# Moving the two halves of x by 64 bytes in SBUF, in a one-core transformer kernel

## The chip, the core and the metric

One NeuronCore of a Trainium2 chip runs the whole program in one launch. The metric is device microseconds from start to end of the program, the median of several executions. Before the change it is 1319.07 us (three executions, 1317.32 to 1320.37).

## What is computed

The input is 256 tokens of 1024 features in float32. Eight layers follow one another: two hybrid blocks ("b1": four mixers beside each other), and then twice a feed-forward layer ("f1"), a second kind of mixer block ("mix") and another feed-forward layer ("f2"). Each reads the normalised x, multiplies it by a large weight matrix, does its own work on the result, multiplies that by a second matrix and adds it to x. Cut to what matters:

```
for l in range(2):
    x = x + mixers(rmsnorm(x) @ w_in[l]) @ w_out[l]          # "b1", w_in 1024 x 3584, w_out 1024 x 1024
x = rmsnorm(x)
for l in range(2):
    h = rmsnorm(x);  x = x + (silu(h @ wg) * (h @ wu)) @ wd   # "f1", wg, wu 1024 x 2816, wd 2816 x 1024
    x = x + mixers2(rmsnorm(x) @ w_in_2[l]) @ w_out_2[l]      # "mix"
    h = rmsnorm(x);  x = x + (silu(h @ wg) * (h @ wu)) @ wd   # "f2"
```

## The kernel before

x stays in SBUF with features on the partitions: `x[P, 8, 256]`, where block k holds features 128k to 128k+127 of all 256 tokens. For the products, float32 values are split into two float32r halves, a high and a low one: x into `xh` and `xl`, the weights into `wh` and `wl`, the hidden layer of a feed-forward layer into `hh` and `hl`, the mixers' outputs into `y1`, `y2` and `y2r` (two tiles each). Every product is then three matmuls: high by high, and high by low both ways.

The weights come in 409 units of 128 x 1024 values, in the order of their use, through `wraw` (5 buffers). ScalarE writes `wh` of a unit (line 882), VectorE `wl` (line 1261); there are 6 buffers of each. TensorE then uses the unit's two tiles of 128 x 512 in one of three forms:

- **Token form** (`project_tokens`, lines 457 to 459), the first product of "b1" and "mix": a 128 x 128 block of `xh` or `xl` is stationary and 512 columns of `wh` or `wl` move. 56 tiles a phase, four phases.
- **Feature form** (`project_features`, lines 473 to 475), the first product of a feed-forward layer: 128 x 128 of `wh` or `wl` is stationary and the 256 columns of `xh` or `xl` move. 88 tiles a phase, four phases.
- **Out form** (`project_out`, lines 488 to 490), the second product everywhere: 128 x 128 of `wh` or `wl` is stationary and 256 columns of `hh` or `hl` (44 tiles a phase), or of the mixers' `y` tiles (16 tiles a phase), move.

Feature form and out form issue the same three matmuls in the same order (high by high, then low moving, then `wl` stationary); 12 of them to a tile. A stationary operand that a matmul needs is loaded by a separate weight load (PEld in the profile), which runs while the matmul before it streams. Each engine's program is one fixed list; semaphores alone tie them together. Between the tiles TensorE also does the mixers' small matmuls and transposes (line 531), the sums of squares for the norms (line 544) and, in "mix", eight pairs of matmuls with the forget gate's weights (lines 733 and 734: `xh` and `xl` move, a slice of `ffw` is stationary that begins 32 bytes further on for each pair).

The tiles lie in SBUF one after the other in the order of the `sb(...)` calls, each start rounded up to 32 bytes. In bytes from the start of a partition, taken from the built programs:

```
tile            before   mod 128  mod 256    after    mod 128  mod 256
wraw             16512       0      128      16512        0      128
wh               36992       0      128      36992        0      128
wl               61568       0      128      61568        0      128
x                86144       0      128      86144        0      128
xh               94336       0      128      94400       64      192
xl              102528       0      128     102592       64      192
cst             110720       0      128     110848        0        0
ffw             123552      32      160     123680       32       32
hh, y1, y2      133184      64       64     133312       64      192
y2r             149568      64       64     149696       64      192
hl              155712      64       64     155840       64      192
```

Within a tile, the slices of the big products begin at multiples of 512 bytes, so that a tile's remainder is that of every operand taken from it.

Of the kernel before, what the change touches and what calls it, by code (L numbers as in the profile page):

```python
# [13 lines left out]
P = 128  # L14
# [175 lines left out]
def program(nc, x_in, w_in, par_in, cst_in, lev_in, msk_in, pos_in, rpb_in, lng_in, lnb_in, out):  # L190
    ctx = ExitStack()

    def sb(name, shape, dt=F32, where=None):
        return (where or ctx).enter_context(nc.sbuf_tensor("s_" + name, shape, dt))
# [5 lines left out]
    wh = sb("wh", [P, NS, UNIT], F32R)  # L200
    wl = sb("wl", [P, NS, UNIT], F32R)
    x = sb("x", [P, 8, TOKENS])
    xh = sb("xh", [P, 8, TOKENS], F32R)
    xl = sb("xl", [P, 8, TOKENS], F32R)
    cst = sb("cst", [P, NCST])
    par = sb("par", [P, NPAR])
    mlev = sb("mlev", [P, NLEV], F32R)
# [2034 lines left out]
```

How the kernel before makes its waits and increments, by code:

```python
        def claim(n, name):  # L440
            b, before = plan[n, name]
            if before:
                pe.wait_ge(emptied[b], before)
            return pb[b]
# [1 line left out]
        def project_tokens(n, tile, c, k):  # L446
            u, j = divmod(tile, TPU)
            s = u % NS
            hi, lo = (w[:, s, NCOL * j:NCOL * (j + 1)] for w in (wh, wl))
            if j == 0 or u < SPLIT_UNITS:
                pe.wait_ge(low_done, piece_of(tile))
            if c == 0:
                pe.wait_ge(xl_done, x_parts(n) + k + 1)
            for t in range(2):
                ts = slice(P * t, P * (t + 1))
                o = (claim(n, ("in", c, t)) if k == 0 else psum(n, ("in", c, t)))[:, :]
                pe.matmul(o, xh[:, k, ts], hi, start=k == 0, stop=False)
                pe.matmul(o, xh[:, k, ts], lo, start=False, stop=False)
                pe.matmul(o, xl[:, k, ts], hi, start=False, stop=k == 7).then_inc(main_done, 1)
# [1 line left out]
        def project_features(n, tile, c, k):  # L461
            u, j = divmod(tile, TPU)
            s = u % NS
            if j == 0 or u < SPLIT_UNITS:
                pe.wait_ge(low_done, piece_of(tile))
            if c == 0:
                pe.wait_ge(xl_done, x_parts(n) + k + 1)
            for i in range(2):
# [9 lines left out]
        def project_out(n, tile, q, pair, first, last):  # L478
# [1 line left out]
            s = u % NS  # L480
            if j == 0:
                pe.wait_ge(low_done, piece_of(tile))
            o2 = claim(n, ("out", q)) if first else psum(n, ("out", q))
```

## Time and profile before

| | |
|---|---|
| median of three executions | 1319.07 us |
| the profiled execution's own time | 1318.59 us |
| its span, first to last instruction | 1316.8 us |
| TensorE busy | 1295.8 us, 98% of the span |
| TensorE's weight loads busy | 1219.4 us, 93% |
| VectorE busy | 900.4 us, 68% |
| ScalarE busy | 709.4 us, 54% |
| mean granted TensorE clock | 0.995 of full |

The profiled execution is 0.48 us under the median, and 1.8 us of its time lie outside the span. A matmul's row gives a modelled length (0.28 us for 256 columns) that overlaps the next matmul's, so TensorE's pace is not read from lengths but from how far apart the starts lie, or from how many matmuls fall in a stretch of known length.

### The profile page before, as it was taken

What the parts mean: (1) busy time and instruction counts of PE and PEld (TensorE: products, weight loads), DVE (VectorE), ACT (ScalarE), POOL (GpSimd) and SP (SyncE); (2) the same over time, 40 slices, a digit from 0 to 9 for tenths busy, and PEclk for the clock granted to TensorE, in tenths of its full rate; (3) what the DMA queues carried; (4) which work ended last, traced back from release to release, by engine and by line L of the source; (5) the groups of instructions that cost most, each with busy time, mean ns of one, the idle gap of its engine ahead of it and who ended that gap; (6) DMA issues with size and microseconds to landing.
All of it is one profiled execution on the core that took longest, in us unless ns stands there. A gap on an engine that the chain in (4) does not pass through costs nothing.

```text
span 1316.8 us, 23603 instructions
## 1 busy us (share of the span) xinstructions
PE 1295.8 (98%) x9662; PEld 1219.4 (93%) x9662; DVE 900.4 (68%) x1588; ACT 709.4 (54%) x1149; POOL 157.6 (12%) x207
## 2 busy tenths in 40 slices
PE   9999999999999999999999999999999999999997
PEld 7788878999999988899999999999998889999997
DVE  6988798867665577767666566666547876766652
ACT  7664665645454485556444544444458546544441
POOL 3201500382001100012000020000110001200000
PEclk9999999999999999999999999999999999999999
DMA  8635644555556552335555555555645133655560
GB/s 313 202 103 177 215 144 129 176 186 175 182 178 195 175 176 79 122 120 193 179 191 192 177 192 184 186 192 181 200 148 185 59 133 126 197 176 183 188 195 34
DMA packets 61499, 221.77 MB, mean 168 GB/s; under 512 B 7120, under 2 KB 7376, under 8 KB 61136
## 3 DMA queue, kind: packets, MB, share of 16 engines
q1 hardware_dynamic: 60768, 219.00, 50.3%
q8 instruction: 76, 1.25, 0.4%
q0 software_dynamic: 336, 1.11, 0.3%
q14 instruction: 31, 0.25, 0.1%
q10 hardware_dynamic: 288, 0.16, 0.1%
HBM read 219.20 MB, written 1.05 MB: 167 GB/s over the span
## 4 chain that ended last, share of the span: by engine, by line
PE 81%; DVE 10%; issue 3%; POOL 3%; ACT 1%; DMA 1%; SPq 0%; DVEq 0%; ACTq 0%; POOLq 0%
PE pb L473 13%; PE pb L475 13%; PE pb L474 13%; PE pb L488 7%; PE pb L490 7%; PE pb L489 7%; PE pb L457 5%; PE pb L459 5%; PE pb L458 5%; DVE s_wl L1261 3%; DVE s_acc L1394 2%; PE pb L531 2%; PE pb L581 2%; PE pb L704 1%; PE pb L560 1%
## 5 line engine op out<-in xcount | busy, mean ns | idle before, releaser
L1261 DVE TENSOR_TENSOR s_wl<-s_wraw,s_wh 128x1024 fp32r<-128x1024 f32 (+1 forms) x411 | 503.5, 1245 | 115.1 <-ACT s_wh L882 114.8
L882 ACT ACTIVATE s_wh<-s_wraw 128x1024 fp32r<-128x1024 f32 (+1 forms) x411 | 420.9, 1048 | 201.6 <-PE pb L475 113.2
L473 PE MATMUL pb<-s_xh,s_wh 128*128 128x256 f32 x1408 | 399.8, 284 | 0.0
L475 PE MATMUL pb<-s_xh,s_wl 128*128 128x256 f32 x1408 | 399.1, 283 | 0.0
L474 PE MATMUL pb<-s_xl,s_wh 128*128 128x256 f32 x1408 | 399.0, 283 | 0.0
L473 PEld LDWEIGHTS pb<-s_xh,s_wh 128*128 128x128 f32 x1408 | 271.0, 192 | 0.0
L474 PEld LDWEIGHTS pb<-s_xl,s_wh 128*128 128x128 f32 x1408 | 271.0, 192 | 0.0
L475 PEld LDWEIGHTS pb<-s_xh,s_wl 128*128 128x128 f32 x1408 | 270.9, 192 | 0.0
L488 PE MATMUL pb<-s_hh,s_wh 128*128 128x256 f32 x704 | 194.6, 276 | 0.0
L489 PE MATMUL pb<-s_hl,s_wh 128*128 128x256 f32 x704 | 194.5, 276 | 0.0
L490 PE MATMUL pb<-s_hh,s_wl 128*128 128x256 f32 x704 | 194.5, 276 | 0.0
L457 PE MATMUL pb<-s_wh,s_xh 128*128 128x512 f32 x448 | 183.0, 409 | 1.9 <-DVE s_wl L1261 1.9
L459 PE MATMUL pb<-s_wh,s_xl 128*128 128x512 f32 x448 | 175.9, 393 | 0.0
L458 PE MATMUL pb<-s_wl,s_xh 128*128 128x512 f32 x448 | 175.6, 392 | 0.0
L1598 DVE TENSOR_TENSOR s_gu<-pb,s_rbc 128x512 f32<-128x512 f32 x88 | 60.8, 691 | 116.9 <-PE pb L475 112.4
L489 PEld LDWEIGHTS pb<-s_hl,s_wh 128*128 128x128 f32 x704 | 132.3, 188 | 0.0
L488 PEld LDWEIGHTS pb<-s_hh,s_wh 128*128 128x128 f32 x704 | 132.2, 188 | 0.0
L490 PEld LDWEIGHTS pb<-s_hh,s_wl 128*128 128x128 f32 x704 | 132.2, 188 | 0.0
L457 PEld LDWEIGHTS pb<-s_wh,s_xh 128*128 128x128 f32 x448 | 84.7, 189 | 20.7 <-DVE s_wl L1261 3.1
L459 PEld LDWEIGHTS pb<-s_wh,s_xl 128*128 128x128 f32 x448 | 84.4, 188 | 18.4
L458 PEld LDWEIGHTS pb<-s_wl,s_xh 128*128 128x128 f32 x448 | 84.8, 189 | 14.9
L1070 ACT ACTIVATE s_sg<-s_gu 128x256 f32<-128x256 f32 x88 | 36.7, 420 | 86.2 <-DVE s_gu L1598 86.0
(302 smaller groups left out, 1515.6 us busy)
## 6 DMA issues: line engine op xcount, KB each, us to landing
s_wraw<-in_w SPq DMA_DIRECT2D x407, 512.0 KB, 4.0
s_nab<-in_rpb SPq DMA_DIRECT2D x2, 1024.0 KB, 8.0
s_x<-in_x SPq DMA_DIRECT2D x4, 256.0 KB, 5.9
out_dram<-s_at_s SPq DMA_DIRECT2D x4, 256.0 KB, 2.3
s_cst<-in_cst SPq DMA_DIRECT2D x1, 684.0 KB, 10.3
s_mlev<-in_lev POOLq DMA_DIRECT2D x1, 576.0 KB, 5.3
s_wraw<-in_w SPq DMA_DIRECT2D x2, 256.0 KB, 4.6
s_ln<-in_lng POOLq DMA_DIRECT2D x2, 128.0 KB, 6.3
```

What stands on the lines that cost most here:

```text
L457: pe.matmul(o, xh[:, k, ts], hi, start=k == 0, stop=False)
L458: pe.matmul(o, xh[:, k, ts], lo, start=False, stop=False)
L459: pe.matmul(o, xl[:, k, ts], hi, start=False, stop=k == 7).then_inc(main_done, 1)
L473: pe.matmul(o, wh[:, s, w], xh[:, k, :], start=k == v == 0, stop=False, skip_group_check=True)
L474: pe.matmul(o, wh[:, s, w], xl[:, k, :], start=False, stop=False, skip_group_check=True)
L475: r = pe.matmul(o, wl[:, s, w], xh[:, k, :], start=False, stop=k == 7, skip_group_check=True)
L488: pe.matmul(o, wh[:, s, w], ah, start=first and m == v == 0, stop=False, skip_group_check=True)
L489: pe.matmul(o, wh[:, s, w], al, start=False, stop=False, skip_group_check=True)
L490: r = pe.matmul(o, wl[:, s, w], ah, start=False, stop=last and m == 1, skip_group_check=True)
L882: return act.activation(o, src, ACT.Copy, scale=scale)
L1261: dve.tensor_tensor(wl[:, s, part], wraw[:, r, part], wh[:, s, part].bitcast(F32), ALU.subtract).then_inc(low_done, 1)
L1598: dve.tensor_tensor(gu[:, j, :, :], psum(n, ("in", c, j))[:, :].rearrange("p (a b) -> p a b", a=2), rbc[:, RBC_SLOT[n], :].unsqueeze(1).to ...
```

## The change

Two unused tiles of 64 bytes a partition are put in, one ahead of `xh`, one behind `xl`.

```diff
     x = sb("x", [P, 8, TOKENS])
+    sb("gap0", [P, 16])
     xh = sb("xh", [P, 8, TOKENS], F32R)
     xl = sb("xl", [P, 8, TOKENS], F32R)
+    sb("gap1", [P, 16])
     cst = sb("cst", [P, NCST])
```

`xh` and `xl` then begin 64 bytes further on, everything behind them 128 bytes further on; the table above has both. No instruction, semaphore or DMA is added, removed or moved: on each of the five engines the two built programs list the same instructions in the same order, with the same shapes.

## Rows read from the trace of the kernel before

**Rows 1.** The page's head and its part 1, busy time of each engine

```profile
span 1316.8 us, 23603 instructions
PE 1295.8 (98%) x9662; PEld 1219.4 (93%) x9662; DVE 900.4 (68%) x1588; ACT 709.4 (54%) x1149; POOL 157.6 (12%) x207
```

**Rows 2.** The page's part 5: one group of each form

```profile
L473 PE MATMUL pb<-s_xh,s_wh 128*128 128x256 f32 x1408 | 399.8, 284 | 0.0
L488 PE MATMUL pb<-s_hh,s_wh 128*128 128x256 f32 x704 | 194.6, 276 | 0.0
L457 PE MATMUL pb<-s_wh,s_xh 128*128 128x512 f32 x448 | 183.0, 409 | 1.9 <-DVE s_wl L1261 1.9
```

**Rows 3.** Windows, TensorE alone: length, busy (matmuls touching it), clock, DMA, GB/s

```profile
280.00:388.00 108.00, 108.00 (x903) 1.00 0.55 182
610.00:723.00 113.00, 113.00 (x944) 1.00 0.56 185
389.00:448.00 59.00, 59.00 (x523) 1.00 0.60 192
725.00:783.00 58.00, 58.00 (x514) 1.00 0.62 194
```

**Rows 4.** Timeline of TensorE where a feature stretch ends: start, length, instruction

```profile
388.35 0.28 PE L474 MATMUL pb<-s_xl,s_wh 128*128 128x256 f32 x1
388.47 0.28 PE L475 MATMUL pb<-s_xh,s_wl 128*128 128x256 f32 x1
388.59 0.29 PE L488 MATMUL pb<-s_hh,s_wh 128*128 128x256 f32 x1
...
389.07 0.28 PE L489 MATMUL pb<-s_hl,s_wh 128*128 128x256 f32 x1
389.18 0.28 PE L490 MATMUL pb<-s_hh,s_wl 128*128 128x256 f32 x1
```

**Rows 5.** Windows, TensorE alone, in out form: three mixer stretches, the last feed-forward

```profile
239.00:251.00 12.00, 12.00 (x108) 1.00 0.82 254
122.00:134.00 12.00, 12.00 (x104) 1.00 0.64 216
1109.00:1118.00 9.00, 9.00 (x79) 1.00 0.52 168
1297.30:1305.80 8.50, 8.50 (x75) 1.00 0.00 0
```

**Rows 6.** Windows of all engines: busy of PE, PEld, DVE, ACT, POOL

```profile
8.00:109.00 101.00, 97.51 (x500) 80.24 (x499) 86.36 (x186) 65.14 (x118) 17.32 (x22) 0.99 0.59 201
449.00:568.00 119.00, 118.81 (x668) 98.80 (x667) 86.35 (x255) 74.61 (x132) 7.40 (x10) 1.00 0.37 122
610.00:723.00 113.00, 113.00 (x944) 113.00 (x943) 73.55 (x98) 56.09 (x81) 0.00 (x0) 1.00 0.56 185
```

**Rows 7.** Timeline of TensorE in token form, in the first "mix"

```profile
481.95 0.39 PE L458 MATMUL pb<-s_wl,s_xh 128*128 128x512 f32 x1
482.17 0.39 PE L459 MATMUL pb<-s_wh,s_xl 128*128 128x512 f32 x1
482.40 0.39 PE L457 MATMUL pb<-s_wh,s_xh 128*128 128x512 f32 x1
```

**Rows 8.** Timeline of TensorE in the forget gate's matmuls, about the fourth and eighth pair

```profile
452.68 0.28 PE L734 MATMUL pb<-s_xl,s_ffw 128*128 128x256 f32 x1
452.79 0.28 PE L733 MATMUL pb<-s_xh,s_ffw 128*128 128x256 f32 x1
452.91 0.28 PE L734 MATMUL pb<-s_xl,s_ffw 128*128 128x256 f32 x1
...
453.62 0.29 PE L734 MATMUL pb<-s_xl,s_ffw 128*128 128x256 f32 x1
453.75 0.28 PE L733 MATMUL pb<-s_xh,s_ffw 128*128 128x256 f32 x1
453.87 0.28 PE L734 MATMUL pb<-s_xl,s_ffw 128*128 128x256 f32 x1
```

## The prediction

> **What bounds the kernel now.** I read the page's busy times first: TensorE is busy for 1295.8 of 1316.8 us [rows 1], so the end is set by TensorE's pace and little else. A change that moves no instruction can then act in one way only, by the distance between successive matmul starts. Those distances come from windows: length of a stretch that holds nothing but one form, over the matmuls in it. A window counts all matmuls that touch it, and since a modelled length of 0.28 us spans more than two distances, some 2.5 too many.
>
> Feature form (`xh`, `xl` move, weights stationary): 108.00 us over 903 - 2.5, and 113.00 over 944 - 2.5, give 119.9 and 120.0 ns [rows 3]. Out form of the feed-forward layers (`hh`, `hl` move, weights stationary): 59.00 over 523 - 2.5, and 58.00 over 514 - 2.5, give 113.4 ns for both [rows 3]. Both stream 256 columns against the same weight tiles, in the same order, with the same number of loads. The timeline at the end of a feature stretch shows the switch in place: 0.12 us between starts while `xl` and `xh` move, 0.12 and a little more for some matmuls about the switch, then 0.11 [rows 4]. No other engine's wait explains it, since TensorE is busy throughout on either side. What differs is where the moving operand lies: `xh` and `xl` begin at remainder 0 of 128 bytes as `wh` and `wl` do, `hh` and `hl` at 64. While one matmul streams its moving operand, the weight load of the next reads its stationary one (both are busy in all of the 113 us [rows 6]), so two reads of SBUF run beside each other all the time, and their remainders decide how they meet. That reading is mine from the comparison; no row isolates it.
>
> **How well does the remainder order the rows?** The mixers' out form (`y1`, `y2`, `y2r`, also at 64) shows two paces with the same addresses: 12 us over 108 - 2.5 is 113.7 ns in one stretch, but 12 over 104 - 2.5 and 9 over 79 - 2.5 are 118.2 and 117.6 ns in two others, and the last feed-forward layer, after an interruption by the norm's sums, ends at 8.5 over 75 - 2.5, 117.2 ns [rows 5]. So 64 apart does not give one pace but a fast pattern (113.3) and a slow one (about 117.7), and which of them holds depends on how the stretch was entered. 0 apart has shown 120 alone.
>
> **The change, term by term.** It adds nothing to any engine, so the whole sum is distances.
>
> 1. Feature form: 3 lines of 1408 [rows 2], 4224 matmuls. After the change they stand to the weights as `hh` does by the remainder of 128. Nearest row: 113.3. 4224 x (120.0 - 113.3) = 28.2 us. Bounds: 117.7 gives 4224 x 2.3 = 9.7 us, 120.0 gives nothing. Some ten matmuls after each interruption aren't in a pattern, which is under 1 us in all and left out. I take 28.2.
> 2. Out form: `hh` and `y` keep their remainder of 128, so by that nothing changes. But today each feature stretch's 120 breaks up at the switch and the out stretch then finds the fast pattern [rows 4]. With no change of remainder at the switch, an out stretch inherits whatever pattern the feature stretch had. All fast: 0. If a whole feed-forward layer sits in the slow one, its out form loses 528 x (117.7 - 113.3) = 2.3 us, and its feature form gains 1056 x 2.3 ns = 2.4 us instead of 7.1: such a layer gives nothing in sum.
> 3. Token form: 3 lines of 448, 1344 matmuls of 512 columns [rows 2]; weights (remainder 0) move, `x` (0 before, 64 after) is stationary. Steady distances are 0.22 to 0.23 us, 482.17 less 481.95 and 482.40 less 482.17 [rows 7]. If the gain per weight load is that of the feature form, 6.7 ns, it is 1344 x 6.7 = 9.0 us at most. In "b1" VectorE is busy for 86.4 of 101 us and TensorE has 3.5 us idle [rows 6], so VectorE's chain of work keeps most of a gain there; in "mix" TensorE is busy for 118.81 of 119 [rows 6] and a gain counts: 612 matmuls x 6.7 = 4.1 us, less what small matmuls interrupt. I take 3 us, between 0 (and a loss of the same size, since no row has 512 columns at 64 apart) and 9.
> 4. Other work: what feeds the faster TensorE must keep up. A unit of weights in feature form takes 24 x 120 = 2.88 us and would take 2.72, as out form does already with 192 to 194 GB/s [rows 3]. VectorE is busy for 73.55 of 113 us there, ScalarE for 56.09 [rows 6]; 6% less time makes that 69% and 53%. Neither becomes the bound, and their operands in `xh`, `xl` get the remainder that `hh`, `hl` have. The forget gate's 32 matmuls are too few to count.
>
> Sum: 1318.59 - 28.2 - 3 = 1287.4 us for an execution like the profiled one; the median stands 0.5 us higher, so 1288 us.
>
> The Trainium skill's "SBUF — State Buffer", "Who interferes with whom", gives TensorE two read ports, one for the moving operand and one for weight loads, as independent, and says that TensorE never waits on anyone; its specifications put the only penalty at 16-byte lines, which a shift by 64 bytes does not touch. By it the sum would be 1319 us. The trace disagrees as far as the 120 against 113.4 ns of [rows 3] come from the operands' place, which it does not prove.
>
> **The rivals.**
>
> A, the likeliest: remainder of 128 decides, all four feature stretches fall in the fast pattern: 1288 us. For it: in each of the four feed-forward layers the out form at 64 found the fast pattern as soon as x was done.
>
> B: the same rule, but one to three of the layers run in the slow pattern. By term 2 each costs 7.1 us: 1295, 1302, 1309 us. For it: three of four stretches in [rows 5] are slow, and a feature stretch is entered from mixer work and interrupted by the norm's sums and transposes, as those were.
>
> C: no effect, 1319 us. Either the place doesn't matter, and 120 against 113.4 belongs to something else that differs between the forms (which PSUM tile is filled, how often a semaphore is set), or all four layers are slow. This is where the page's rule leads, worked here as 0 x 4224. Against its first half: the split at the switch is abrupt, and 120 appears only with x moving.
>
> D, slower: what decides is the remainder of 256, not 128. Then the gap behind `xl` is harmful: everything behind it moves by 128, so `hh`, `hl` and `y`, which stood 64 below the weights' remainder (64 to 128), stand 64 above it (192), where no steady row exists. One pace s would hold for features, outs and y, 7104 matmuls. Before they took 4224 x 120 + 2112 x 113.3 + 768 x about 115.5 ns = 834.9 us; with the 3 us of term 3, it is a loss from s = 837.9 / 7104 = 117.9 ns on. At s = 120 it is 14.6 us, 1333 us. For it: in the forget gate's matmuls the fourth pair's weights lie 128 from x and the eighth's 0, the same remainder of 128; around the fourth the starts are 0.11 and 0.12 apart, around the eighth 0.13 and 0.12 [rows 8], so the two may not be the same thing. Against: these matmuls are a dozen in a row and settle in no pattern.
>
> E: A with token form gaining wherever it can, and mixer stretches fast as well: 9 + 2 us instead of 3, 1280 us.
>
> **How the numbers follow.** A 0.44, B 0.22, C 0.13, D 0.16, E 0.05. Predicted is A, 1288 us; A's own range is 1283 to 1293. The overall range runs from 1281 to 1320: it leaves out D and the outer part of E, about 2 in 10. An effect of under 0.2% of 1319 us, 2.6 us, is about what a measurement can't tell from no change. Faster: A, B, E and a twentieth from C and D near 117 ns, 0.75. Same: most of C, 0.10. Slower: D at over 118, 0.15.
>
> **What the profile after would show.** Right: in a window within a feature stretch, 113 us hold some 1000 matmuls instead of 944, TensorE busy throughout; out stretches hold 8.8 per us as before; token stretches of "mix" shorter by a few us. B: feature windows at 8.5 per us in some layers, and the out stretch behind each such one at 8.5 too. C: 8.33 per us unchanged. D: out stretches with fewer than 8.8 per us in every layer, although `hh` kept its remainder of 128. The prediction is also wrong if a new wait appears on `wl` (line 1261) in the feature stretches, where none was: then the pace came and VectorE didn't follow.

## The result

The changed kernel takes 1307.24 us (median of 4, 1306.01 to 1308.75) against 1319.26 us (4 executions in the same series); the ratio is 0.9917, 95% interval 0.9903 to 0.9930. It is faster, by 12 us where 31 were forecast. Run again in a later series, beside other kernels, it took 1305.18 us (1300.92 to 1306.77), ratio 0.9880 (0.9858 to 0.9902).

The page of the profile after, head and parts 1 and 5 (beside [rows 1, 2]):

```profile
span 1304.2 us, 23603 instructions
PE 1285.9 (99%) x9662; PEld 1204.7 (92%) x9662; DVE 899.3 (69%) x1588; ACT 709.8 (54%) x1149; POOL 156.5 (12%) x207
...
L475 PE MATMUL pb<-s_xh,s_wh 128*128 128x256 f32 x1408 | 391.5, 278 | 0.0
...
L490 PE MATMUL pb<-s_hh,s_wh 128*128 128x256 f32 x704 | 195.4, 278 | 0.0
L459 PE MATMUL pb<-s_wh,s_xh 128*128 128x512 f32 x448 | 184.5, 412 | 1.3 <-DVE s_wl L1263 1.3
```

(Line numbers are two higher than before.) The modelled length of a feature matmul fell from 284 to 278 ns, that of an out matmul, whose addresses keep their remainder of 128, rose from 276 to 278, and the token form's from 409 to 412. Such means hide what happens, since they run over all layers. The windows, TensorE alone, one in the features and one in the outs of each feed-forward layer (beside [rows 3]):

```profile
310.00:380.00 70.00, 70.00 (x597) 1.00 0.56 188
400.00:440.00 40.00, 40.00 (x342) 1.00 0.51 169
640.00:715.00 75.00, 75.00 (x665) 1.00 0.57 192
740.00:775.00 35.00, 35.00 (x311) 1.00 0.61 205
830.00:895.00 65.00, 65.00 (x576) 1.00 0.57 194
915.00:950.00 35.00, 35.00 (x311) 1.00 0.54 171
1150.00:1230.00 80.00, 80.00 (x681) 1.00 0.57 187
1260.00:1290.00 30.00, 30.00 (x257) 1.00 0.18 61
```

Length over the count less 2.5, as in the prediction: layer one 117.7 ns in the features and 117.8 in the outs, layers two and three 113.2 to 113.5 in both, layer four 117.9 in both. 120 ns is gone everywhere. Two layers of four run in the fast pattern and two in the slow one, and within each layer the outs have the pattern of the features. VectorE and DMA kept up: TensorE is busy throughout each window.

The starts tell where a layer gets its pattern. In this profile the features change pace only where the norm's small matmuls interrupt them, behind their 60th and their 84th matmul (in layer one the 84th and the 132nd): layer two enters slow and is fast from the 84th on, layer three is slow from the 60th to the 84th alone, layer four enters fast and is slow from the 60th on, layer one is slow throughout. What holds behind the 84th then holds to the end of the outs.

In token form, the same 119 us as in [rows 6] now hold 662 matmuls instead of 668, again with TensorE busy throughout (118.92 us):

```profile
449.00:568.00 119.00, 118.92 (x662) 98.10 (x661) 86.00 (x254) 74.15 (x132) 7.42 (x10) 1.00 0.36 121
```

Starts in the trace are kept to the nanosecond; in token form the commonest distances were 226 and 227 ns and are now 231 to 236. Leaving out the first six distances after each interruption, the mean rose from 226.8 to 233.3 ns.

### The profile page after: what moved, and what is told of

Read it like the earlier page. It is cut to its first block, busy times and chain, and to the rows that moved or that the text cites. A ratio compares the mean times of both kernels' runs of the same rounds, so it can differ in the third digit from the quotient of the medians.

```text
span 1304.2 us, 23603 instructions
## 1 busy us (share of the span) xinstructions
PE 1285.9 (99%) x9662; PEld 1204.7 (92%) x9662; DVE 899.3 (69%) x1588; ACT 709.8 (54%) x1149; POOL 156.5 (12%) x207
## 4 chain that ended last, share of the span: by engine, by line
PE 83%; DVE 8%; POOL 3%; issue 3%; ACT 1%; DMA 1%; SPq 0%; DVEq 0%; ACTq 0%; POOLq 0%
PE pb L476 12%; PE pb L477 12%; PE pb L475 12%; PE pb L490 7%; PE pb L491 7%; PE pb L492 7%; PE pb L459 6%; PE pb L461 5%; PE pb L460 5%; DVE s_wl L1263 2%; PE pb L533 2%; PE pb L583 2%; DVE s_acc L1396 1%; PE pb L706 1%; PE pb L562 1%
## 5 line engine op out<-in xcount | busy, mean ns | idle before, releaser
L475 PE MATMUL pb<-s_xh,s_wh 128*128 128x256 f32 x1408 | 391.5, 278 | 0.0
L477 PE MATMUL pb<-s_xh,s_wl 128*128 128x256 f32 x1408 | 391.1, 278 | 0.0
L476 PE MATMUL pb<-s_xl,s_wh 128*128 128x256 f32 x1408 | 391.1, 278 | 0.0
L476 PEld LDWEIGHTS pb<-s_xl,s_wh 128*128 128x128 f32 x1408 | 264.4, 188 | 0.0
L475 PEld LDWEIGHTS pb<-s_xh,s_wh 128*128 128x128 f32 x1408 | 264.2, 188 | 0.0
L477 PEld LDWEIGHTS pb<-s_xh,s_wl 128*128 128x128 f32 x1408 | 264.0, 188 | 0.0
```

The source lines that it names most:

```text
L475: pe.matmul(o, wh[:, s, w], xh[:, k, :], start=k == v == 0, stop=False, skip_group_check=True)
L476: pe.matmul(o, wh[:, s, w], xl[:, k, :], start=False, stop=False, skip_group_check=True)
L477: r = pe.matmul(o, wl[:, s, w], xh[:, k, :], start=False, stop=k == 7, skip_group_check=True)
```

## The experiments

Distances below are the windows' or, where three digits are given without a row, means over starts. "Apart" is the address of x, `hh` or `y` less that of the weights, modulo 256 bytes: before, x to weights 0, `hh` and `y` to weights -64; after the change, all of them +64. What stands in brackets holds for the one unit of weights that was moved in each feed-forward layer. No kernel leaves out any of the work. Each profile is of one execution; where it is said which layers were fast, that is known of this one alone.

| run | x to weights | hh, y to weights | us | ratio (95%) |
|---|---|---|---|---|
| the change, again | +64 | +64 | 1305.18 | 0.9880 (0.9858 to 0.9902) |
| rest kept modulo 256 | +64 | -64 | 1319.86 | 1.0011 (1.0000 to 1.0023) |
| rest moved alone | 0 | +64 | 1328.39 | 1.0082 (1.0059 to 1.0104) |
| weights moved | +64 | 0 | 1325.50 | 1.0050 (1.0032 to 1.0068) |
| x by 32 | +32 | +64 | 1310.22 | 0.9939 (0.9924 to 0.9955) |
| xh alone | +64, xl 128 | +64 | 1321.29 | 1.0015 (1.0005 to 1.0025) |
| x below | -64 | -64 | 1304.41 | 0.9889 (0.9856 to 0.9922) |
| unit moved below, all -64 | -64 (0) | -64 | 1316.51 | 0.9977 (0.9966 to 0.9988) |
| unit moved above, all +64 | +64 (0) | +64 | 1300.72 | 0.9851 (0.9830 to 0.9872) |
| unit moved below, all +64 | +64 (128) | +64 | 1320.71 | 1.0013 (1.0004 to 1.0022) |
| unit moved above, all -64 | -64 (128) | -64 | 1294.98 | 0.9827 (0.9806 to 0.9848) |
| unit moved above, and more | 0 in token form, else +64 | +64 | 1295.52 | 0.9817 (0.9803 to 0.9831) |

**The change, again.** Nothing is edited.

> The changed kernel once more, on this chip beside the others. If the pattern of each layer is fixed by the program, two layers of four are fast again and the time is 1307 us; if it is drawn anew by chip or execution, the executions spread in steps of 7 us.

1305.18 us, from 1300.92 to 1306.77. In the profiled execution layers two and three are again fast and layers one and four slow; one execution, at 1300.92, is 3 to 6 us below the rest. That fits a program that mostly, not always, settles which layer gets which pattern; the fast execution was not profiled.

**The rest kept modulo 256.** The edit is against the changed kernel.

```diff
-    sb("gap1", [P, 16])
+    sb("gap1", [P, 48])
```

> The two halves of x 64 bytes further on as in the change, but the gap behind them is 192 bytes, so that all tiles behind keep their remainder of 256 too. Theory 1 (the difference of the two operands' starts modulo 128 decides, and which pattern a stretch falls in depends on its entry): features and outs at 113.3 or 117.7 ns between starts, 512-column matmuls at 233 ns, as after the change; 1300 to 1309 us, about 1307 if the entries draw the same patterns. Theory 2 (the remainder of 256 decides, and the change put hh and y on a worse one): outs back at 113.3 ns in all four feed-forward layers, and the features alone as after the change; about 5 us less than the changed kernel, 1302 us.

1319.86 us. Both theories missed: features and outs are in patterns of 64 apart, no distance of 120, but all four layers are slow. Windows of the first layer and the second, features and outs:

```profile
310.00:380.00 70.00, 70.00 (x596) 1.00 0.56 187
400.00:440.00 40.00, 40.00 (x342) 1.00 0.54 172
640.00:715.00 75.00, 75.00 (x639) 1.00 0.56 187
740.00:775.00 35.00, 35.00 (x299) 1.00 0.50 167
```

75 us over 639 - 2.5 is 117.8 ns. So the 12 us that the change gains hang on which layers are fast, and moving tiles that aren't x's by 128 bytes takes them away. In this kernel the moving address steps by 128 bytes between `y` or `hh` and x, both ways. The starts show the slow pattern right behind each of the eight such boundaries that nothing interrupts, and before two of them, where the second and the fourth layer begin, the pattern was the fast one.

**The rest moved alone.** The edit is against the kernel before.

```diff
     xl = sb("xl", [P, 8, TOKENS], F32R)
+    sb("gap1", [P, 32])
```

> xh and xl stay where they were, and everything behind them moves by 128 bytes. Theory 1 (difference modulo 128): nothing changes, features at 120.0 ns, outs at 113.3 ns in all four layers, 512 columns at 227 ns, 1319 us. Theory 2 (modulo 256): outs are no longer at 113.3 ns in every layer, and the time goes up by 5 us or more.

1328.39 us. The features stay at 120.0 (878 matmuls in 105 us) and token form at 227, but the outs, in all four layers, go from 113.3 to 117.8:

```profile
280.00:385.00 105.00, 105.00 (x878) 1.00 0.54 182
390.00:448.00 58.00, 58.00 (x495) 1.00 0.58 191
```

4 x 528 x 4.4 ns is 9.3 us, against 10.2 us by the medians. Theory 2's forecast for the outs came true and theory 1's failed: at +64 the pace is one of the same two as at -64, but it is not the same one. Before, x to `hh` was a step of the moving address by -64 (modulo 256) and led to fast four times; here it is +64 and leads to slow four times.

**The weights moved instead of x.** The edit is against the kernel before.

```diff
     wraw = sb("wraw", [P, NR, UNIT])
+    sb("gap0", [P, 16])
     wh = sb("wh", [P, NS, UNIT], F32R)
     wl = sb("wl", [P, NS, UNIT], F32R)
+    sb("gap1", [P, 16])
```

> The weights' halves wh and wl begin 64 bytes further on instead of the halves of x; hh, hl and y stay at 64, so that they now stand at difference 0 to the weights. Theory 1 (the difference of the two operands counts): features at 113.3 or 117.7 ns, outs at 120.0 ns in all layers, 512 columns at 233 ns. The outs lose 2112 x 6.7 ns and the mixers' outs 768 x 4 ns, 17 us, against a gain of 10 to 28 in the features and a loss of some 6 in token form: 1314 to 1332 us. Rival (only the moving operand's own place counts): features stay at 120.0, outs stay at 113.3, and the 512 columns, whose weights move, change alone: 1313 to 1325 us.

1325.50 us (1321.31 to 1329.44). The two gaps move the weights by 64 bytes and everything behind them, x included, by 128, so that x comes to +64 and `hh` to 0 from the weights. Theory 1 holds: the features leave 120 though x keeps its remainder of 128, and `hh` takes 120 (294 matmuls in 35 us, 120.1). Windows of the first two layers, features and outs:

```profile
310.00:380.00 70.00, 70.00 (x620) 1.00 0.57 194
400.00:440.00 40.00, 40.00 (x335) 1.00 0.53 178
640.00:715.00 75.00, 75.00 (x639) 1.00 0.54 180
740.00:775.00 35.00, 35.00 (x294) 1.00 0.53 179
```

It is the difference of the two operands that counts, not the place of one: `hh` lies at remainder 192 of 256 here, after the change and in the run with the rest moved alone, and only here, with the weights at 192 too, do its matmuls take 120 ns. The first layer's features are fast (113.4) and the others' slow. The starts show why the others are: each layer's features are entered from 120 ns, by a step of the moving address of +64 (from `y` or `hh` to x), and each begins slow; the first turns fast only behind the interruption at its 132nd matmul. The second layer's entry, in TensorE's timeline:

```profile
593.32 0.28 PE L490 MATMUL pb<-s_y2r,s_wh 128*128 128x256 f32 x1
...
594.76 0.28 PE L475 MATMUL pb<-s_xh,s_wh 128*128 128x256 f32 x1
...
596.18 0.28 PE L475 MATMUL pb<-s_xh,s_wh 128*128 128x256 f32 x1
```

Twelve distances take 1.44 us before the boundary and 1.42 behind it (the fast pattern would take 1.36). The eight executions fall into two groups, 1321.3 to 1323.5 and 1327.5 to 1329.4 us, about as far apart as one layer's features are worth (1056 x 4.4 ns, 4.6 us).

**x by 32 bytes.** The gaps are 8 and 24 floats.

> The halves of x 32 bytes further on, and 96 bytes of gap behind them. Theory 1 has no number for a difference of 32: if two 64-byte halves of a 128-byte line are what counts, 32 lies across both and does no better than 0 (120 ns or more in the features, over 1316 us); if the two reads must only not start on the same place, 32 does as well as 64 (113.3 or 117.7 ns, 1295 to 1309 us).

1310.22 us. The features show patterns of their own, 116.7 ns in the mean in all four layers (645 in 75 us), token form is at 233. Neither of the two ideas: 32 apart is better than 0, and has no fast pattern of 113.3. The outs behind, entered by a step of +32, are slow in the first layer and fast in the other three.

**xh alone.** A gap of 16 floats ahead of `xh` and one between `xh` and `xl`.

> One part of the change alone: xh 64 bytes further on, xl 128, so that xl keeps its remainder of 128 and everything behind xl lies as after the change. Theory 1: matmuls that stream xl beside a load of weights stand at difference 0 and those that stream xh at 64, in a fixed order of two to one; the mean lies between, 115 to 119 ns, and 120 cannot be held in each. 1305 to 1316 us. If only all operands at 64 together allow a fast pattern, 120 ns and 1319 us.

1321.29 us. A steady pattern of three, about 115, 118 and 120 ns, 117.8 in the mean, in all features, and slow outs behind it in all four layers. In the timeline of TensorE:

```profile
340.84 0.28 PE L475 MATMUL pb<-s_xh,s_wh 128*128 128x256 f32 x1
340.96 0.28 PE L476 MATMUL pb<-s_xl,s_wh 128*128 128x256 f32 x1
341.08 0.28 PE L477 MATMUL pb<-s_xh,s_wl 128*128 128x256 f32 x1
341.20 0.28 PE L475 MATMUL pb<-s_xh,s_wh 128*128 128x256 f32 x1
341.31 0.28 PE L476 MATMUL pb<-s_xl,s_wh 128*128 128x256 f32 x1
```

From 340.84 to 341.20, three distances take 0.36 us (3 x 117.8 ns is 0.353, the rows being rounded). The pace is the one that theory 1 gave, the time is not: the slow outs and a token form at 231 ns, neither of them forecast, take back what the features gain. With `xl` at 128 and only `xh` at 64, no feature stretch finds the fast pattern.

**x below the weights.** The gaps are 48 and 16 floats, so that nothing else changes modulo 256.

> xh and xl 192 bytes further on and 256 bytes in all behind them: x stands 64 below the weights modulo 256, where the change puts it 64 above, and hh and y stay 64 below as in the kernel before. Theory 1 (a difference of 64 modulo 128 allows a fast and a slow pattern, and a stretch keeps the one it was entered with, out form inheriting it from the features): features and outs of each feed-forward layer share one pace, 113.3 or 117.7 ns; 1290 us with four fast layers, 1318 us with none, in steps of 7 us. Rival (64 below is the fast side and 64 above the slow one): all features and outs at 113.3 ns, 1290 us.

1304.41 us, executions from 1299.85 to 1308.41. The profiled one has three fast layers and one slow (the third, features 554 in 65 us, outs 300 in 35). Theory 1 holds, the rival is out: 64 below has both patterns, and outs keep what they were entered with. Two executions lie at 1300 and two at 1308, about one layer's worth apart, which fits a draw that differs from one execution to the next.

**One unit of weights moved.** To force the draw, one unit per feed-forward layer lies 64 bytes off (of 408 units in all; the count of 409 in the description of the kernel is one too many). `wh` and `wl` get 64 bytes of room at either end, and gaps keep all else modulo 256.

```diff
+def of_unit(u, a, b):
+    o = 16 + (u % NS) * UNIT + (STEP if u in MOVED else 0)
+    return slice(o + a, o + b)
...
-                    pe.matmul(o, wh[:, s, w], xh[:, k, :], start=k == v == 0, stop=False, skip_group_check=True)
+                    pe.matmul(o, wh[:, w], xh[:, k, :], start=k == v == 0, stop=False, skip_group_check=True)
```

with `w = of_unit(u, ...)`, STEP of -16 or +16 floats, and MOVED the first unit in buffer 0 or in buffer 5 from each layer's eighth on. First, all at -64 and the unit lower:

> e5 and one unit of weights per feed-forward layer, the first in buffer 0 from the layer's eighth unit on, written and read 64 bytes lower, so that its 24 matmuls stand at difference 0 to x. Theory: those 24 settle at 120 ns, and from 120 a stretch 64 below falls into the fast pattern, as the kernel before's outs did four times of four; so from that unit on features and outs run at 113.3 ns in all four layers. About 1291 us (28 us less than before, 3 us back in token form, which goes from 227 to 233 ns). Rival (the pattern is set by something else, and one unit doesn't reset it): layers as in e5.

1316.51 us, and the expectation turned upside down: within the moved unit 120 ns, but behind it slow, in all four layers, also where it was fast before. The unit's end and the slow pattern behind it, in TensorE's timeline:

```profile
297.14 0.28 PE L491 MATMUL pb<-s_xh,s_wh 128*128 128x256 f32 x1
297.26 0.28 PE L492 MATMUL pb<-s_xl,s_wh 128*128 128x256 f32 x1
297.38 0.28 PE L493 MATMUL pb<-s_xh,s_wl 128*128 128x256 f32 x1
...
298.20 0.28 PE L491 MATMUL pb<-s_xh,s_wh 128*128 128x256 f32 x1
298.32 0.28 PE L492 MATMUL pb<-s_xl,s_wh 128*128 128x256 f32 x1
298.44 0.28 PE L493 MATMUL pb<-s_xh,s_wl 128*128 128x256 f32 x1
298.55 0.28 PE L491 MATMUL pb<-s_xh,s_wh 128*128 128x256 f32 x1
```

From 297.26, the first start behind the unit, to 298.55 eleven distances take 1.29 us, 117 ns each. Then the change's own places, and the unit higher:

> The change's own places (x, hh and y 64 above the weights modulo 256) and one unit of weights per feed-forward layer written and read 64 bytes higher, so that its 24 matmuls stand at difference 0. Theory: from 120 a stretch 64 above falls into the slow pattern, as the outs of the run with only the rest moved did four times of four; so features and outs at 117.7 ns in all four layers, about 1321 us. Rival (a reset to 120 always leads to the fast pattern): 1293 us.

1300.72 us: again the opposite, fast behind the unit in all four layers.

```profile
297.10 0.28 PE L492 MATMUL pb<-s_xl,s_wh 128*128 128x256 f32 x1
297.22 0.28 PE L493 MATMUL pb<-s_xh,s_wl 128*128 128x256 f32 x1
297.34 0.28 PE L491 MATMUL pb<-s_xh,s_wh 128*128 128x256 f32 x1
...
298.02 0.28 PE L491 MATMUL pb<-s_xh,s_wh 128*128 128x256 f32 x1
298.13 0.28 PE L492 MATMUL pb<-s_xl,s_wh 128*128 128x256 f32 x1
298.25 0.28 PE L493 MATMUL pb<-s_xh,s_wl 128*128 128x256 f32 x1
298.36 0.28 PE L491 MATMUL pb<-s_xh,s_wh 128*128 128x256 f32 x1
```

From 297.34 to 298.36 nine distances take 1.02 us, 113 ns each. The reset works; my rule for its outcome, taken from where the stretch lies, was wrong. What fits both, and [rows 4] and the runs with the rest moved alone and with the weights moved, is the step by which an operand's address changes at the boundary: `hh` after x was -64 and fast, +64 and slow; x after `hh` or `y` +64 and slow; the weights after the moved unit +64 and slow, -64 and fast. Place and step can be pulled apart with the same unit moved to the other side.

> x, hh and y 64 above the weights modulo 256 as in the changed kernel, but the moved unit lies 64 bytes lower, so that the weights come back by a step up. Theory of the step (down leads to the fast pattern, up to the slow one): slow in all four layers after the moved unit, outs at 117.7 ns, about 1318 us. Rival (the place decides: 64 above is fast after a reset, 64 below slow): fast, outs at 113.3 ns, about 1300 us. Both want the moved unit itself (128 bytes apart) to run at 120.0 ns, if only the remainder of 128 counts for that.

> x, hh and y 64 below the weights modulo 256, and the moved unit 64 bytes higher, so that the weights come back by a step down. Theory of the step: fast in all four layers after the moved unit, outs at 113.3 ns, about 1298 us (token form at 229.6 ns as in the other runs with x there). Rival (the place decides): slow as in the run with the unit moved below, 1316 us.

1320.71 us, slow in all four layers, and 1294.98 us, fast in all four. The windows of the first and the third layer, features and outs, unit lower and all +64:

```profile
310.00:380.00 70.00, 70.00 (x597) 1.00 0.56 188
400.00:440.00 40.00, 40.00 (x342) 1.00 0.52 168
830.00:895.00 65.00, 65.00 (x554) 1.00 0.55 182
915.00:950.00 35.00, 35.00 (x299) 1.00 0.59 195
```

and unit higher and all -64:

```profile
310.00:380.00 70.00, 70.00 (x620) 1.00 0.57 194
400.00:440.00 40.00, 40.00 (x356) 1.00 0.60 196
830.00:895.00 65.00, 65.00 (x576) 1.00 0.58 195
915.00:950.00 35.00, 35.00 (x311) 1.00 0.63 206
```

The step decides and the place does not. The sign was tied to the buffer in these four kernels (the lower unit is in buffer 0, the higher in buffer 5), but that isn't it: in the run with the weights moved, layers begin at the change from buffer 5 to buffer 0, the same as behind the higher unit, and there the step is +64 and leads to slow. The 1294.98 us are a median of four, and one of the four, at 1300.52, is 5 to 7 us above the rest and was not profiled; so that the reset holds in every execution isn't shown. One part of the expectation failed: at 128 apart the moved unit doesn't hold 120 but a pattern of five (115, 117, 122, 120, 119), 118.7 ns in the mean. So 0 and 128 apart are not quite the same thing, as [rows 8] had hinted.

**More units moved, and x at 0 for token form.** `xh` and `xl` become one flat tile with 64 bytes of room, read and written from its start in "b1" and "mix" and 64 bytes further on in the feed-forward layers; all units in buffer 5 in the mixers' outs and at the start of the features are moved too.

> The run with a unit moved above, and two things more: x's halves begin at difference 0 to the weights in b1 and mix (token form) and 64 above in the feed-forward layers; and every unit in buffer 5 is moved in the mixers' out stretches and at the start of the features. Theory (a step of one operand down by 64 bytes out of the 120 ns pattern leads to the fast one, a step up to the slow one; token form at difference 0 takes 227 ns): 1300.7 us less 4 us in token form and less about 2 us of slow stretches, 1295 us. If the layers' patterns are drawn anew all the same, 1298 to 1312 us.

1295.52 us, as forecast: token form back at 227, and the features behind the last moved unit at 113.3. The moved units in the mixers' outs reset the pattern too, but brought nothing in sum: the out stretches average 118.3, 118.0, 118.3 and 115.7 ns, moved units, interruptions and the slow pattern that follows some of these together, against 117.8, 117.8, 113.8 and 117.8 in the run with one unit moved above. One boundary went against the rule: unit 167, in the second mixer's outs, ran at 0 apart in a turn of 117, 118, 121, 120 and 124 ns, 120.0 in the mean too, and a step of -64 out of that led to slow. So 0 apart has two patterns of one mean, and only out of the constant 120 did the step decide. The time equals that of the simpler kernel of the run before it (1294.98), whose token form at -64 takes 229 ns. Either is some 10 us faster than the change.

## Why the prediction was wrong

**The bound and the two paces: right.** TensorE's distances set the end, no other engine or DMA came in the way, no wait on `wl` appeared in the features, and 120 ns was the price of two operands 0 apart. The run with the weights moved shows that the difference counts.

**The step that failed: taking 113.3 ns for all 4224 matmuls of term 1.** Its ground stood under rival A: "in each of the four feed-forward layers the out form at 64 found the fast pattern as soon as x was done". True, but it found it because of how it was entered, from 120 ns by a step of -64; the run with the rest moved alone has the same features, the step +64, and slow outs in all layers. The change takes both the 120 and the step away, so the four cases of the fast pattern were no evidence for it. Term 2 had said as much ("inherits whatever pattern the feature stretch had"), and rival B with two slow layers is what came: 1302 us by its price, and the 6 us between the gain that term 3 gave and the loss that came make it 1308. B had a chance of 0.22; the three stretches of four in [rows 5] near 117.7 ns deserved more weight than the four feed-forward outs at 113.3.

**Term 1 as measured:** the two layers at 113.3 ns give 2 x 1056 x 6.7 = 14.2 us, the two at 117.8 give 2 x 1056 x 2.3 = 4.9, together 19 for 28.2. By the starts, from a layer's first feature matmul to its last, layers two and three are 6.8 and 6.9 us shorter, layer four 1.9 and layer one 3.9, of which 1.5 are not the change's (see the sum).

**Term 2:** two slow layers' outs lose 2 x 528 x 4.4 = 4.6 us, for 0 (by the starts 2.3 and 1.9; the last layer's outs had been slow in part before).

**Term 3 had the wrong sign.** I took 3 us of gain from the thought that what a weight load gains beside 256 columns it also gains beside 512. It is the other way: at +64, 233.3 for 227 ns, at -64, 229. In each "mix" 6 matmuls fewer fit into 119 us, and by the starts each is 1.0 us longer; of the two "b1" one is 1.1 us longer and one 0.4 shorter, 2.6 us lost in all. (The two "mix" hold 2 x 336 = 672 matmuls in token form, not 612; the term was taken at 3 us, so nothing hangs on it.) The text had named a loss of this size, and that no row had 512 columns at 64 apart.

**The sum:** 19 - 4.6 - 2.6 is 11.8 us of gain; the medians say 12.0, the two profiled spans 12.6. Of the latter 1.5 us aren't the change's: before, TensorE's granted clock fell for 3 to 4 us near the start of the first feed-forward layer, right after TensorE had stood still for 1.7 us in the norm's sums, and 15 matmuls there start 213 ns apart for 120. In the profile after the clock is 1.00 in that place. TensorE alone, before:

```profile
270.00:274.00 4.00, 4.00 (x22) 0.57 0.88 277
274.00:280.00 6.00, 6.00 (x53) 1.00 0.46 162
```

**Rival C** is out in its first half: the place matters. Its second half, all four layers slow at 1319 us, is what the run with the rest kept modulo 256 shows (1319.86). The Trainium skill's "SBUF — State Buffer", "Who interferes with whom", with its two independent read ports of TensorE, would have no change at all; the trace disagrees, by 12 us here and by 33 us between the slowest and the fastest of these kernels, which issue the same instructions on all engines.

**Rival D** was right in that a remainder of 256 plays a part and that moving `hh` by 128 can do harm (10 us in the run with the rest moved alone), and wrong in how: it sets no one pace for 64 above, it sets the step.

**The range** held the time, since it was drawn to hold B and C too; the gain was 12 us for 31.

## What to carry to other kernels

Where matmuls with fresh weight loads run back to back, compare the distance between their starts by form before anything else: here 6% lay between two forms, and the runs trace it to the addresses' remainders. A pattern seen at one place of a kernel is evidence for another only if it is entered in the same way; look at what preceded it, and at all stretches with the same addresses, before one pace is multiplied by thousands. A gain that depends on such a draw can be lost to any later edit that moves a tile; a short stretch that resets it, here 24 matmuls at 64 bytes off and a step back down, fixed it in every feed-forward layer of the three kernels that had it, in the execution of each that was profiled.

## What the runs showed that I had not expected

- With 256 columns of float32r and a 128 x 128 float32r load for each, there are steady patterns: 120.0 ns at 0 apart; 113.3, or 118, 118 and 117 in turn, at +64 and at -64; a turn of five, 118.7 in the mean, at 128 (seen over 24 matmuls at a time); a mixture, 116.7 in the mean, at +32. The others last over hundreds of matmuls, until something interrupts them or an address steps. With 512 columns and x stationary: 227 with x at the weights' remainder, 226, 229 and 232 in turn with x 64 below, 233.3 with x 64 above.
- Out of the constant 120 ns or the turn of five at 128 apart, a step of one operand by -64 bytes led to the fast pattern at 24 uninterrupted boundaries of 24 (4 before the change, 4 each with the unit higher, 12 with more units moved), one by +64 to the slow one at 16 of 16 (4 each with the rest moved alone, with the weights moved, and with the unit lower in two kernels), whichever operand made the step and on whichever side of the other it ended. A step of the moving operand by 128, from 64 on one side of the weights to 64 on the other, led to slow at 8 of 8. Out of the other turn at 0 apart, the one boundary seen went to slow after -64. Why the sign matters is open. That two reads meet in some part of SBUF fits, with a period of 256 bytes, but no run measured that by itself; and why an interrupted stretch falls into one pattern or the other, mostly alike in every execution of a program and now and then not, was not found.
